# Sliding-window masks in a fused VectorE operation per head, and two branch weight blocks split by ScalarE and GpSimd

## The reference

```python
scores = jnp.einsum("bnqhgd,bnkhd->bnhgqk", qb, kw) * (A_HEAD_DIM ** -0.5)
band = (rel >= 0) & (rel < WINDOW)                 # WINDOW = 128
scores = jnp.where(valid[None, :, None, None], scores, -jnp.inf)
mx = jnp.maximum(jnp.max(scores, axis=-1, keepdims=True), sink)
pr = jnp.exp(scores - mx)
den = jnp.sum(pr, axis=-1, keepdims=True) + jnp.exp(sink - mx)
attn = pr / den
out = jnp.einsum("bnhgqk,bnkhd->bnqhgd", attn, vw)
...
merged = sigmoid(g_m) * (hm @ w_branch_m) + sigmoid(g_a) * (ha @ w_branch_a)
h = h + merged @ w_out
```

## Time and profile before

| | |
|---|---|
| median of three runs | 2620.47 us (2618.46 to 2623.45) |
| profiled execution, its own time | 2622.02 us |
| its span | 2620.0 us |
| TensorE busy | 2570.6 us, 98% |
| VectorE busy | 1994.7 us, 76% |
| ScalarE busy | 606.4 us, 23% |
| GpSimd busy | 138.9 us, 5% |
| granted TensorE clock, mean | 0.996 of full speed |

### The profile page before, as it was taken

One profiled execution on the slowest core, in us unless ns is written; L12 is line 12 of the kernel. 1 busy time (PEld: TensorE's weight loads), 2 busy tenths in 40 slices (PEclk: granted clock), 3 DMA queues, 4 the chain that ended last, 5 costly groups with the idle time before them and its releaser, 6 DMA issues.

```text
span 2620.0 us, 31732 instructions
## 1 busy us (share of the span) xinstructions
PE 2570.6 (98%) x13004; PEld 2107.0 (80%) x13004; DVE 1994.7 (76%) x2296; ACT 606.4 (23%) x1282; POOL 138.9 (5%) x105
## 2 busy tenths in 40 slices
PE   6999999999999999999999999999999999999999
PEld 3788888888877876899788888788888888878887
DVE  4788786978657657977877888777687778978776
ACT  2111111311222147222210332410121023242101
POOL 0000000000002012200200002010000000100000
PEclk8999999999999999999999999999999999999999
DMA  7542342444544633655655545365565555444653
GB/s 273 183 155 97 106 140 72 144 149 161 177 160 130 205 82 81 194 183 175 213 180 168 190 160 179 117 203 171 176 202 184 177 185 178 145 144 162 203 181 121
DMA packets 253103, 426.10 MB, mean 163 GB/s; under 512 B 35728, under 2 KB 93520, under 8 KB 252448
## 3 DMA queue, kind: packets, MB, share of 16 engines
q1 hardware_dynamic: 248352, 410.09, 48.2%
q0 software_dynamic: 3088, 8.75, 1.1%
q10 hardware_dynamic: 1520, 5.25, 0.7%
HBM read 420.89 MB, written 3.16 MB: 162 GB/s over the span
## 4 chain that ended last, share of the span: by engine, by line
PE 90%; DVE 5%; ACT 3%; DMA 1%; issue 1%; ACTq 0%; POOL 0%; DVEq 0%
PE psum L515 86%; PE psum L529 2%; DVE wgt_lo L1810 2%; PE psum L861 1%; DVE wgt_hi L1808 1%; DMA raw<-ada_w 1%; ACT W L1239 1%; ACT L1239 0%; ACT xh L1239 0%; DVE xl L1831 0%; DVE W L2298 0%; ACT n_prob_b L1239 0%; DMA cst<-consts 0%; DVE xl L1819 0%; ACT psum L1239 0%
## 5 line engine op out<-in xcount | busy, mean ns | idle before, releaser
L1810 DVE TENSOR_TENSOR wgt_lo<-raw,wgt_hi 128x2048 fp32r<-128x2048 f32 (+1 forms) x332 | 752.7, 2267 | 11.4
L515 PE MATMUL psum<-wgt_hi,xh 128*128 128x512 f32 (+1 forms) x1744 | 682.7, 391 | 2.8 <-DVE wgt_lo L1810 2.0
L515 PE MATMUL psum<-wgt_hi,xl 128*128 128x512 f32 (+1 forms) x1744 | 676.0, 388 | 0.0
L515 PE MATMUL psum<-wgt_lo,xh 128*128 128x512 f32 (+1 forms) x1728 | 669.3, 387 | 0.0
L1808 DVE CAST wgt_hi<-raw 128x2048 fp32r<-128x2048 f32 (+1 forms) x332 | 406.5, 1224 | 125.0 <-PE psum L515 116.1
L515 PEld LDWEIGHTS psum<-wgt_hi,xh 128*128 128x128 f32 x1744 | 327.5, 188 | 74.0 <-issue 5.7
L515 PEld LDWEIGHTS psum<-wgt_hi,xl 128*128 128x128 f32 x1744 | 327.4, 188 | 66.2
L515 PEld LDWEIGHTS psum<-wgt_lo,xh 128*128 128x128 f32 x1728 | 324.7, 188 | 62.3
L515 PE MATMUL psum<-wgt_hi,yh 128*128 128x512 f32 x928 | 364.8, 393 | 1.4 <-DVE wgt_lo L1810 1.0
L515 PE MATMUL psum<-wgt_hi,yl 128*128 128x512 f32 x928 | 361.6, 390 | 0.0
L515 PE MATMUL psum<-wgt_lo,yh 128*128 128x512 f32 x928 | 361.4, 389 | 0.0
(11 more groups left out here) (242 smaller groups left out, 2203.7 us busy)
## 6 DMA issues: line engine op xcount, KB each, us to landing
raw<-mlp_w SPq DMA_DIRECT2D x64, 1024.0 KB, 5.3
raw<-w_in SPq DMA_DIRECT2D x60, 1024.0 KB, 5.0
raw<-ada_w SPq DMA_DIRECT2D x48, 1024.0 KB, 5.3
raw<-ffn_w_gate SPq DMA_DIRECT2D x40, 1024.0 KB, 5.1
raw<-ffn_w_up SPq DMA_DIRECT2D x40, 1024.0 KB, 5.1
raw<-ffn_w_down SPq DMA_DIRECT2D x40, 1024.0 KB, 5.1
raw<-ret_w_in SPq DMA_DIRECT2D x24, 1024.0 KB, 5.1
raw<-nat_w_in SPq DMA_DIRECT2D x12, 1024.0 KB, 5.5
```

The costliest lines, as they stand in the source:

```text
L515: return pe.matmul(o, l, r, start=start_, stop=stop, skip_group_check=True)
L1810: v.tensor_tensor(wgt_lo[:, s % RING, :size], r, wgt_hi[:, s % RING, :size], ALU.subtract).then_inc(split_done.sem, split_done.up())
```

## The change

Three things are changed in each of the two hybrid layers, and one follows from them.

First, the mask matmuls are gone: the first matmul of each head opens its own sum. The mask is now read where it was loaded (`tri`), so the copy of it into `xh` is gone too. Second, `rowmax` issues one `tensor_tensor_reduce` per head in place of one reduction per bank: it adds the mask to the scores, writes them back to PSUM and gives the maximum. Third, blocks ba1 and ba2 (numbers 1 and 2 in the order of "ba") become side blocks: ScalarE converts ba1 between ahigh(0) and softmax(3), and ba2 between ahigh(2) and aturned(5); GpSimd subtracts both. `side_blocks` becomes a dictionary by layer and name so that the two can be found; for the four older side blocks nothing moves.

```diff
@@ tokens_by_features
+                    if b in side:
+                        now["side"] = (name, b)
                     wh, wl, n = take_block(pe, mkblock(k0, kn_, col0 + (chunks[c] if chunks else c) * BANK, BANK),
                                            parts(c) if stacked else ())
@@ ascores
                     outs = [open_unit(pe, ("as", n, j), "soft") for j in range(2)]
-                    mask = a_mask[:, P - qt * P:2 * P].unsqueeze(1).to_broadcast([P, nh // 2, w_])
-                    for o in outs:
-                        mm(o.rearrange("p (h k) -> p h k", h=nh // 2), ident_r, mask, True, False)
...
-                            ins = mm(o[:, k * w_:(k + 1) * w_], qT[p0:p0 + AHD, h // 2, qt * P:(qt + 1) * P], kT[p0:p0 + AHD, h // 4, 0:w_], False, True)
+                            ins = mm(o[:, k * w_:(k + 1) * w_], qT[p0:p0 + AHD, h // 2, qt * P:(qt + 1) * P], kT[p0:p0 + AHD, h // 4, 0:w_], True, True)
@@ the branch product
-                                   order=[(0, 0), (1, 0), (0, 1), (1, 1)], each=in_branch)
+                                   order=[(0, 0), (1, 0), (0, 1), (1, 1)], each=in_branch, side=(1, 2))
@@ ScalarE
                 ahigh(0)
+                side_cast(now["layer"], ("ba", 1))
                 softmax(3)
...
                 ahigh(2)
+                side_cast(now["layer"], ("ba", 2))
                 aturned(5)
@@ VectorE
-                v.tensor_copy(a_mask, tri[:, P:3 * P])
...
-                        ins = v.tensor_reduce(small[:, 96 + c0 + j:96 + c0 + j + nh - 1:2], bank_of(("as", n, j)).rearrange("p (h k) -> p h k", h=nh // 2),
-                                              AX, ALU.max)
+                        for k in range(nh // 2):
+                            x = bank_of(("as", n, j))[:, k * w_:(k + 1) * w_]
+                            c = 96 + c0 + 2 * k + j
+                            ins = v.tensor_tensor_reduce(x, x, mask, 1.0, -3e38, ALU.add, ALU.max, small[:, c:c + 1])
@@ GpSimd
+                for b in (1, 2):
+                    side_low(i + 1, ("ba", b))
                 pool.wait_ge(psum_full.sem, filled(("mg", 3)))
```

More of the change, by code:

```diff
@@ L241, in build @@
         units = {}
-        blocks, split_blocks, asked, side_blocks = [], [], [], []
+        blocks, split_blocks, asked, side_blocks = [], [], [], {}
         ada_blocks = []
@@ L291, in ask_block @@
             if side:
-                side_blocks.append(s)
+                side_blocks[now["layer"], side] = s
             done = (side_split, len(side_blocks)) if side else (split_done, s + 1 - len(side_blocks))
@@ L413, in build @@
         a_spread, a_inv = U[:, 0, 0:BANK], [U[:, 0, BANK:2 * BANK], U[:, 1, 0:BANK]]
-        a_mask, ident_r = xh[:, 6, T:2 * T], xh[:, 7, T:T + P]
+        a_mask, ident_r = tri[:, P:3 * P], xh[:, 7, T:T + P]
         ones = small[:, 331:332]
@@ L533, in tokens_by_features @@
             def tokens_by_features(name, kts, col0, ncols, tts, oh, ol, owner, mkblock, split_k=None, after=None, ready=None, mid=None,
-                                   each=None, chunks=None, order=None, late=None, parts=None):
+                                   each=None, chunks=None, order=None, late=None, parts=None, side=()):
                 split_k = split_k or [(k, min(4, kts - k)) for k in range(0, kts, 4)]
@@ L698, in ple_product @@
                     pe.wait_ge(out_of(("pT",)), emptied(("pT",)))
-                    now["side"] = True
+                    now["side"] = "pp"
                     seen["pp", i] = take_block(pe, lblock(a["ple_proj_w_2"], 0, 2, 0, D))
@@ L829, in _ @@
             ready = turn_normed("h1", 4, lambda: ple_product(1, p_tiles[2:]), (6, 7))
-            now["side"] = True
+            now["side"] = "nk"
             features_by_tokens("nk", D, KT, 2 * T, "act", wb, after=lambda b: ask_modulation(1, 5, b), ready=ready)
@@ L1029, in hybrid_layer @@
                     ple_product(0, p_tiles[3:])
-                    now["side"] = True
+                    now["side"] = "fg"
                 feed_forward(1, pairs_of("f1"), mid=(lambda: turn_next(i, 1)) if i else None, after=lambda: turn_x("mx", (0, 1), after=(("fd", 1), 0, 1)))
@@ L1330, in mlp, with side_cast @@
                     mod_row(1, 3, 4)
-                for s in side_blocks[2 * layer:2 * layer + 2]:
-                    side_cast(s)
+                side_cast(2 - layer, "pp")
+                side_cast(layer, ("nk", "fg")[layer])
                 ple_out(1 - layer, p_tiles[:2 + layer])
-            def side_cast(s):
+            def side_cast(layer, name):
+                s = side_blocks[layer, name]
                 b = split_blocks[s]["block"]
@@ L2476, in rowmax @@
                     hs = slice(c0 - 16 * qt, c0 - 16 * qt + nh)
+                    w_, mask = P * (qt + 1), a_mask[:, P - qt * P:2 * P]
                     for j in range(2):
@@ L2641, in load_p, with side_low @@
                 pool.dma_start(l_p, a["p_2"][i][0].rearrange("(t p) n -> p t n", p=P)).then_inc(p_in.sem, p_in.up())
-            def side_low(s):
+            def side_low(layer, name):
+                s = side_blocks[layer, name]
                 b = split_blocks[s]["block"]
@@ L2665, in _ @@
             add_window(0)
-            for s in side_blocks[0:2]:
-                side_low(s)
+            side_low(2, "pp")
+            side_low(0, "nk")
             ln_rstd(4)
@@ L2680, in _ @@
             load_vectors(0)
-            for s in side_blocks[2:4]:
-                side_low(s)
+            side_low(1, "pp")
+            side_low(1, "fg")
             ln_rstd(2)
```

## The result

The changed kernel takes 2630.0 us (2627.96 to 2630.9) beside 2619.06 us of the kernel before in the same session: ratio 1.0036, 95% interval 1.0025 to 1.0046. By the ratio that is 9.4 us more (6.5 to 12.0); the two medians lie 10.9 apart. The forecast was 2631.

What follows compares the result with a forecast made beforehand. TensorE's matmuls and a ScalarE/VectorE chain were taken to bound the stage together; 3.6 us at softmax(3) plus 1.75 at ba2 is 5.35 a layer, 10.7 in all, so 2631 us, range 2621.5 to 2636.5.

Steps and rivals of the forecast that it cites:

- ScalarE's chain as the second bound: Attention stage up to ba0: ScalarE and VectorE work without a gap from 1656.75 to 1680.72, ending together with TensorE's matmuls.
- the masks' 3.6 us: Six pairs of mask matmuls a layer leave TensorE, 0.60 us each; all given back by waiting at item 4's scores.
- third rival: ScalarE's chain isn't the bound up to ba0; TensorE keeps all 3.6 us a layer: 2613.3 us, chance 0.09.
- GpSimd's start: GpSimd begins subtracting ba1 at 1666.15, after ScalarE's conversion, and runs until 1670.8.
- The hold: At rowmax(3), VectorE's two small operations wait until GpSimd's whole subtraction ends; softmax(3) and ba0 come 3.6 us later.
- second rival: No wait at rowmax(3) or ba3's split, GpSimd late or VectorE early: -0.7 us a layer, 2619 us, chance 0.09.
- The fused operations: On VectorE in rowmax: 0.29 us each at 128 columns, 0.42 at 256; +1.1 us an item of eight, +0.5 of four.
- ba2: GpSimd's subtraction of ba2 holds VectorE's split of ba3 2.4 us; alow(3) ends late, so ba2 waits 1.75 us more a layer.
- TensorE's clock: After waiting about 5 us at item 4's scores TensorE may drop to its lower level: at most 2.8 us a layer, chance 0.10.
- inner bounds of the sum: Unknown prices of fused operations and GpSimd's length in both layers: 5.0 to 6.8 us a layer, 2630.5 to 2634 us.
- first rival: Only conversions and copies out of SBUF stand still, rowmax(3)'s small operations don't: +1.05 us a layer, 2622.6 us, chance 0.12.

Runs made afterwards that it cites:

- the square above: Kernel before; before with gate (1,1)'s sigmoid later on ScalarE; before with only the masks fused; before with both: ratios 1, 0.9998, 0.9987, 0.9979.
- the gate's move: Sigmoid and table load of gate (1,1) put behind aturned(3), ahigh(1) and ainverse(2) on ScalarE: 0.9998 in the kernel before, 0.9979 with masks fused.

## Why the prediction was right, step by step

- **ScalarE's chain as the second bound**: right. The claim that the masks' 3.6 us are all given back held in after, and the square above (0.3 and 1.0 us alone, 2.9 together) bears out that TensorE and ScalarE's chain ended close together before. The third rival's condition, slack in that chain, can be made (by the gate's move) but wasn't there.
- **GpSimd's start**: worked out as 28.27 us into the stage (1666.15 - 1637.88), measured 28.35. Its length was 4.53 and 4.57, taken as 4.63.
- **The hold**: right in mechanism, and a little off in the operation. I had both small operations wait and counted 0.43 us for them behind GpSimd's end. The first slipped in 0.16 us ahead of GpSimd, only the second waited, and its end met GpSimd's. So softmax(3) came 3.24 us later, not 3.6, and ba0 3.33. That a hold came at all was partly luck. The sum gave GpSimd a lead of 0.25 us over both operations; measured, it led the second by 0.04 and 0.01 us in the two layers of the profiled execution. Had VectorE got there first, the hold would most likely have fallen on an operation behind rowmax(3), much as where GpSimd was made to wait (ratio 1.0003, no change), which is close to the second rival's answer. The profiled execution, held in both layers, is the fastest of the six; how the others fell no trace shows.
- **The fused operations** were priced too high: 0.25 and 0.38 us from start to start, not 0.29 and 0.42. The read of the accumulator is free, the lower of the bounds that I gave. I took it that this hardly matters at rowmax(3). But the eight took 2.12 us up to the first small operation, not 2.3, rowmax(3) began 0.15 us sooner in the stage than worked out, and GpSimd 0.08 later. Together that is 0.41 us, more than the lead of 0.25 that I had given GpSimd, and so the first small operation slipped in.
- **ba2** was the term that was mis-sized: +1.21 and +1.28 between ba0 and the merge for 1.75. VectorE's conversion of ba3 was due 9.33 us after ba0, as worked out (9.3); but GpSimd was through with ba2 11.19 us after ba0, not 11.7. The conversion took 2.94 us where 1.22 is usual, so it was held for 1.7 us, not 2.4: its last 1.08 us lie behind GpSimd's end. (So do those of the row at 918.00, 922.32 - 921.24, which I read as 1.2.) I had moved ScalarE's conversion of ba2 by 0.5 for rowmax(5), which grew by 0.34, had let it start behind ahigh(2)'s end where it started 0.14 us ahead of it, and had taken GpSimd's slower duration.
- **TensorE's clock**: after the wait of 4.80 us it did fall, to 0.54 in the stretch below. I gave that a chance of 0.10 and up to 2.8 us. It cost 0.1 us at most: the matmuls from item 4's scores on took 2.3 us longer in the first layer, but ScalarE's chain covered that almost exactly. Its last link, alow(1), ended at 1680.74, and ba0 started at 1680.98 without a wait, 13.24 us after softmax(3), before 13.15. In the second layer, at 0.69 from 2349.5 to 2355, ba0 still waited 0.17 us for alow(1).

```profile
1665.00:1670.00 5.00, 0.51 (x2) 0.53 (x4) 4.01 (x5) 2.26 (x14) 2.69 (x1) 0.78 0.30 72
1670.00:1675.00 5.00, 5.00 (x22) 2.73 (x19) 2.40 (x11) 4.95 (x10) 0.00 (x0) 0.54 0.45 173
```

Two errors of the same sign, 0.3 at ba0 and 0.5 at ba2, make 1.6 us in two layers. That is the distance of 10.7 to the 9.1 of the traces. The measured 4.54 and 4.57 us a layer lie below the inner bounds of the sum, 5.0 to 6.8, and 2630.0 just below their 2630.5. Those bounds were also added up wrongly: 5.35 less 0.15 is 5.2, and with 0.4 and 1.4 on top it is 7.15. The stated range, which reaches down to the first rival, holds the result.

## What to carry to other kernels

Before giving work to GpSimd, list what VectorE does while it runs: an operation of a tenth of a us with both inputs in SBUF, or a copy inside SBUF, waits for GpSimd's whole instruction if that has started first, and if it stands on the chain the chain waits too. When a stage has two bounds that end together, take a little off both: here each alone gave 0.3 and 1.0 us, both together 2.9.

## What was not expected of the hardware

- VectorE's add with maximum out of PSUM starts every 0.25 us at 128 columns and 0.38 at 256, its accumulator read of 0.14 us wholly beside the next one.
- What GpSimd holds up is narrower than "VectorE": held were additions and other small operations on SBUF tiles (4.50, 1.05), a copy inside SBUF (4.54) and conversions; not held were a reciprocal (0.20), copies out of PSUM (0.68, the one at 1667.51 above) and the fused operations.
- The same wait of 1.63 us was followed by the lower granted clock (0.66) in one layer of one execution and not in the other, and so was the wait of 2.03 us where GpSimd was made to wait (0.67 and 1.00). What decides it is left open; it was not tried.
